# A two-stack decoder kernel in split float32r: both parts of the normed input placed at the far end of SBUF

## The chip, the cores and the metric

One core of one Trainium2 chip runs the whole program. The metric is device time in microseconds (us). A core has five engines that run their own instruction streams and meet at semaphores: TensorE (PE in the rows; its weight loads are listed apart as PEld), VectorE (DVE), ScalarE (ACT), GpSimd (POOL) and SyncE (SP), which here issues the DMAs. SBUF is the on-chip memory, 128 partitions wide; every tensor has one start address, a number of bytes inside each partition. PSUM is the small memory that TensorE writes its products to.

## The reference, cut to what matters

256 tokens of width 1024 pass through one block of a first kind (norm, input projection, a state-space mixer and banded attention side by side, output projection, then a second norm and 128 x 128 experts in the dense form below) and two blocks of a second kind (norm, projection, sparse and latent attention, output projection, then a second norm and a feed-forward part of width 4096). What is computed is set by lines such as these:

```python
def rms_norm(x, g):
    r = lax.rsqrt(jnp.mean(xf * xf, axis=-1, keepdims=True) + RMS_EPS)
    return (xf * r).astype(x.dtype) * g

proj = xn @ w_in[layer]                       # first block
h = h + (g_s5 * y_s5 + g_attn * y_attn) @ w_out[layer]
a = jnp.einsum('cd,ced->ce', xb, u_tab[eb])   # experts, up
w = gb * jax.nn.gelu(a, approximate=False)
return jnp.einsum('ce,ced->cd', w, v_tab[eb]) # experts, down
```

All inputs and outputs are float32.

## The kernel before, in words

**The split products.** A float32 product is made as three float32r products: with x = xh + xl and w = wh + wl (high part rounded, low part the rest) it adds xh·wh, xl·wh and xh·wl in one PSUM bank. A float32r matmul here takes a 128 x 128 stationary operand (loaded by an LDWEIGHTS) and streams a moving operand of 256 or 512 columns against it. In `pe.matmul(out, a, b)` the first operand, `a`, is stationary and the second, `b`, is moving. A row of a matmul names the moving operand first: `ps<-xh,wl` streams `xh` against weights from `wl`, `ps<-wh,xh` streams `wh` against a chunk of `xh` that has been loaded as the stationary operand.

**The tensors.** `xh` and `xl` hold the two parts of a normed input, 8 chunks of 256 tokens each. `wh` and `wl` hold two units each of the rounded weights and their rests. `slots` holds four units of 512 KB as they come from HBM. `early_hi` and `early_lo` (placed over the start of the arena) hold the input of the experts' query projection before its norm is applied. `mix_hi`, `mix_lo`, `hidden_hi` and `hidden_lo` are the same kind of pairs for the mixers' outputs and for the feed-forward's hidden layer. `arena` (131072 bytes per partition) holds everything else of the first block; the second kind of block lays `layer`, `mix_hi`, `mix_lo`, `hidden_hi`, `hidden_lo` and `y_out` over the same place.

**The stages, in order of the span.** 0 to 266 us: the first block's projections and mixers (`pair_product`, L537, with `xh`/`xl` moving, and with `early_hi`/`early_lo` moving from 241 us on). 266 to 653 us: 128 expert rows "up" (`up_row`, L2638, L2639 and L2643: 24 matmuls of 256 columns each, `xh`/`xl` moving). 653 to 1022 us: 128 expert rows "down" (`down_row`, L2660 and L2667: 12 matmuls of 512 columns each, `wh`/`wl` moving and a chunk of `xh`/`xl` stationary). Then twice: projections (`split_pair`, L2028, `xh`/`xl` moving), attention, `branch` (L2086, L2091), the feed-forward's up part (L2028 again) and its down part (L2329, `hidden_hi`/`hidden_lo` moving).

**The order of the work.** Every engine's stream is written out by hand, with explicit semaphores. For each unit of weights SP issues a DMA into a slot, ACT rounds it into `wh` (L184, L2376), POOL subtracts to get `wl` (L199, L2438), and PE uses the two and frees them. Nothing in this order depends on where a tensor stands.

**The placement.** Tensors are placed from the low end upwards in the order of the code, each start rounded up to a multiple of 32 bytes. The starts that matter (bytes in a partition), with the remainder by 64:

```
tensor       start    bytes    start mod 64
slots        24704    16384      0
xh           59936     8192     32
xl           68128     8192     32
wh           76320     8192     32
wl           84512     8192     32
early_hi     96832     8192      0
early_lo    105024     8192      0
mix_hi      120384     8192      0
mix_lo      128576     8192      0
hidden_hi   136768    32768      0
hidden_lo   169536    32768      0
```

A chunk of 256 tokens is 1024 bytes, so all chunks of one tensor have the remainder of its start. `xh` to `wl` stand at remainder 32 because `layer_par`, just below them, has 4056 bytes.

Of the kernel before, what the change touches and what calls it, by code (L numbers as in the profile page):

```python
# [20 lines left out]
F32R = mybir.dt.float32r  # L21
# [4 lines left out]
P = 128  # L26
T = 256
TT = T // P
D = 1024
DC = D // P  # L30
# [240 lines left out]
def build(nc, stop_after, xT, consts, par1, bias1, w1, keys, wu, wv, par2, w2, out):  # L271
    ctx = ExitStack()
    with ctx:
        def sb(name, cols, dt=F32):
            return ctx.enter_context(nc.sbuf_tensor(name, [P, cols], dt))
# [8 lines left out]
        small = sb("small", 2304)  # L284
        layer_par = sb("layer_par", LAYERS * NPAR2)

        xh, xl = sb("xh", DC * T, F32R), sb("xl", DC * T, F32R)
        wh, wl = sb("wh", 2 * SLOT, F32R), sb("wl", 2 * SLOT, F32R)
        eps, std, rst = sb("eps", 4), sb("std", T), sb("rst", T)
        row0_hi, row0_lo = (sb(n, T, F32R)[:, :] for n in ("row0_hi", "row0_lo"))  # L290
# [2608 lines left out]
```

## Time and profile before

| | |
|---|---|
| median of 3 runs | 1713.44 us (1713.36 to 1714.88) |
| profiled execution | 1710.85 us, of which span 1709.0 us |
| PE busy (matmuls) | 1638.6 us, 96% |
| PEld busy (weight loads) | 1502.8 us, 88% |
| DVE / ACT / POOL busy | 882.5 / 925.0 / 1196.7 us |
| granted TensorE clock | 0.995 of full speed |
| DMA | 280.42 MB, mean 164 GB/s |

The span runs from the first to the last instruction. Matmuls overlap each other: one lasts 280 to 400 ns by itself, while the next one starts some 120 or 227 ns after it. So the pace is read from the starts of rows in the timeline (the start of one row to the start of the next, divided by the count of the first row), or from the chain of waits, where a piece lasts until the next one begins.

### The profile page before, as it was taken

The numbers are of one execution on the slowest core, as the hardware profiler recorded it, in microseconds if no ns is written. First come the engines' busy times: TensorE is split into PE (matmuls) and PEld (weight loads), VectorE is DVE, ScalarE is ACT, GpSimd is POOL, SyncE is SP. The second block draws the span as 40 slices with busy tenths as digits, with TensorE's granted clock in tenths as the row PEclk, the third lists the DMA queues.
The fourth block names the chain that finished last, engine by engine and source line by source line (L and its number), as shares of the span: only waits on it lengthen the run. The fifth ranks groups of instructions, "written<-read, shape, count | busy, mean of one in ns | idle before, by whom it ended". The sixth has DMA issues, their size and how long they took to land.

```text
span 1709.0 us, 32062 instructions
## 1 busy us (share of the span) xinstructions
PE 1638.6 (96%) x12800; PEld 1502.8 (88%) x12800; DVE 882.5 (52%) x1817; ACT 925.0 (54%) x1553; POOL 1196.7 (70%) x500
## 2 busy tenths in 40 slices
PE   8988999999999999999999999998999998999997
PEld 7876999999999998888888888777999986789997
DVE  6988446992366667777611115876220168752101
ACT  6666655445444445555566655665553447655533
POOL 5552777888877777777888887125888762268885
PEclk9999999999999999999999999999999999999999
DMA  7431555565555555555566664513656644145663
GB/s 263 126 123 54 190 168 169 173 192 180 181 165 170 166 172 166 175 177 174 192 195 189 195 197 136 183 52 116 190 181 188 189 149 162 51 148 185 183 188 112
DMA packets 79891, 280.42 MB, mean 164 GB/s; under 512 B 8704, under 2 KB 9472, under 8 KB 79488
## 3 DMA queue, kind: packets, MB, share of 16 engines
q1 hardware_dynamic: 79744, 278.38, 52.3%
q8 instruction: 102, 1.67, 0.4%
q14 instruction: 45, 0.37, 0.1%
HBM read 277.30 MB, written 1.05 MB: 163 GB/s over the span
## 4 chain that ended last, share of the span: by engine, by line
PE 84%; DVE 6%; issue 4%; ACT 3%; POOL 2%; DMA 0%; POOLq 0%; DVEq 0%; SPq 0%; ACTq 0%
PE ps L2660 14%; PE ps L2028 13%; PE ps L2329 10%; PE ps L2638 7%; PE ps L2639 7%; PE ps L2643 7%; PE ps L2667 7%; PE ps L537 6%; POOL wl L199 2%; ACT wh L184 1%; PE ps L2624 1%; PE ps L2626 1%; PE ps L371 1%; PE ps L2152 1%; PE ps L2122 1%
## 5 line engine op out<-in xcount | busy, mean ns | idle before, releaser
L199 POOL TENSOR_TENSOR wl<-slots,wh 128x1024 fp32r<-128x1024 f32 x236 | 572.7, 2430 | 355.8 <-ACT wh L184 339.9
L2438 POOL TENSOR_TENSOR wl<-slots,wh 128x1024 fp32r<-128x1024 f32 x256 | 619.2, 2420 | 141.4 <-ACT wh L2376 139.3
L2376 ACT ACTIVATE wh<-slots 128x1024 fp32r<-128x1024 f32 x256 | 271.4, 1060 | 367.8 <-issue 237.1
L184 ACT ACTIVATE wh<-slots 128x1024 fp32r<-128x1024 f32 x236 | 249.6, 1060 | 259.7 <-PE ps L2329 105.5
L2638 PE MATMUL ps<-xh,wh 128*128 128x256 f32 x1024 | 253.7, 285 | 0.0
L2639 PE MATMUL ps<-xl,wh 128*128 128x256 f32 x1024 | 250.8, 283 | 0.0
L2639 PEld LDWEIGHTS ps<-xl,wh 128*128 128x128 f32 x1024 | 196.2, 192 | 0.0
L2638 PEld LDWEIGHTS ps<-xh,wh 128*128 128x128 f32 x1024 | 196.0, 191 | 0.1
L2660 PE MATMUL ps<-wh,xh 128*128 128x512 f32 x508 | 159.3, 395 | 0.0
L2660 PE MATMUL ps<-wh,xl 128*128 128x512 f32 x508 | 157.1, 390 | 0.0
L2537 DVE TENSOR_TENSOR small<-ps,small 128x512 f16<-128x512 f32 x128 | 87.7, 685 | 118.6 <-PE ps L2626 118.6
L2643 PE MATMUL ps<-xh,wl 128*128 128x256 f32 x1024 | 143.7, 283 | 0.6 <-POOL wl L2438 0.6
L2564 DVE TENSOR_TENSOR xl<-ps,xh 128x256 fp32r<-128x256 f32 x127 | 53.6, 422 | 167.2 <-ACT xh L2392 167.2
L2667 PE MATMUL ps<-wl,xh 128*128 128x512 f32 x508 | 136.0, 390 | 0.0
L2643 PEld LDWEIGHTS ps<-xh,wl 128*128 128x128 f32 x1024 | 132.1, 192 | 0.8 <-POOL wl L2438 0.8
L2329 PE MATMUL ps<-hidden_hi,wh 128*128 128x256 f32 x512 | 124.3, 280 | 1.9 <-POOL wl L199 1.9
L2329 PE MATMUL ps<-hidden_lo,wh 128*128 128x256 f32 x512 | 124.0, 280 | 0.0
L2667 PEld LDWEIGHTS ps<-wl,xh 128*128 128x128 f32 x508 | 95.4, 188 | 20.4
L2660 PEld LDWEIGHTS ps<-wh,xl 128*128 128x128 f32 x508 | 95.4, 188 | 20.2
L2028 PE MATMUL ps<-xh,wh 128*128 128x256 f32 x704 | 105.7, 289 | 5.5 <-ACT wh L184 3.2
L2660 PEld LDWEIGHTS ps<-wh,xh 128*128 128x128 f32 x508 | 93.2, 188 | 18.0
L2028 PEld LDWEIGHTS ps<-xh,wh 128*128 128x128 f32 x704 | 92.5, 191 | 11.7 <-issue 6.2
(386 smaller groups left out, 3067.5 us busy)
## 6 DMA issues: line engine op xcount, KB each, us to landing
slots<-w SPq DMA_DIRECT2D x260, 512.0 KB, 3.6
slots<-wu SPq DMA_DIRECT2D x128, 512.0 KB, 3.6
slots<-wv SPq DMA_DIRECT2D x128, 512.0 KB, 3.5
arena<-bias SPq DMA_DIRECT2D x1, 2048.0 KB, 8.1
h<-xT SPq DMA_DIRECT2D x4, 256.0 KB, 5.6
arena<-keys SPq DMA_DIRECT2D x1, 1024.0 KB, 8.2
yT<-y_out SPq DMA_DIRECT2D x2, 512.0 KB, 2.7
layer<-consts SPq DMA_DIRECT2D x1, 800.0 KB, 5.3
```

What stands on the lines that cost most here:

```text
L184: act.activation(self.hi[:, n % 2, :], self.slots[:, u % SLOTS, :], ACT.Copy).then_inc(self.rounded, 1)
L199: pool.tensor_tensor(self.lo[:, n % 2, :], self.slots[:, self.order[n] % SLOTS, :], self.hi[:, n % 2, :].bitcast(F32), ALU.subtract).then_ ...
L537: ins = pe.matmul(halves[j], w[:, k, :], x[:, k, :], start=(first and k == 0), stop=(last and k == DC - 1), skip_group_check=True)
L2028: ins = pe.matmul(halves[j], w[:, k, :], x[:, k, :], start=(first and k == 0), stop=(last and k == DC - 1), skip_group_check=True)
L2329: return pe.matmul(out_banks[c // 2][:, (c % 2) * T:(c % 2 + 1) * T], w[:, c * P:(c + 1) * P], x[:, u, :], start=start, stop=False, skip_g ...
L2376: act.activation(whv[:, r % 2, :], slots_v[:, r % SLOTS, :], ACT.Copy).then_inc(w_hi, 1)
L2438: pool.tensor_tensor(wlv[:, r % 2, :], slots_v[:, r % SLOTS, :], whv[:, r % 2, :].bitcast(F32), ALU.subtract).then_inc(w_lo, 1)
L2638: pe.matmul(out, hi[:, k, :], xhT[:, k, :], start=(k == 0), stop=False)
L2639: ins = pe.matmul(out, hi[:, k, :], xlT[:, k, :], start=False, stop=False)
L2643: ins = pe.matmul(out, lo[:, k, :], xhT[:, k, :], start=False, stop=(k == DC - 1))
L2660: ins = pe.matmul(psum[2 * t + half], part_a[:, tokens], hi[:, half * 512:(half + 1) * 512], start=begins, stop=False, skip_group_check=True)
L2667: ins = pe.matmul(psum[2 * t + half], a_hi[:, t * P:(t + 1) * P], lo[:, half * 512:(half + 1) * 512], start=False, stop=(row == NE2 - 1), ...
```

## The change

`xh` and `xl` are allocated from the other end of SBUF. Nothing else in the code changes.

```diff
-        xh, xl = sb("xh", DC * T, F32R), sb("xl", DC * T, F32R)
+        xh, xl = (ctx.enter_context(nc.sbuf_tensor(n, [P, DC * T], F32R, side="right")) for n in ("xh", "xl"))
         wh, wl = sb("wh", 2 * SLOT, F32R), sb("wl", 2 * SLOT, F32R)
```

What stood above `xl` moves down by 16384 bytes, and the two tensors fill the last 16384 bytes:

```
tensor       start before   start now   mod 64 before, now   mod 128 before, now
xh              59936        221152          32, 32               32, 96
xl              68128        212960          32, 32               32, 96
wh              76320         59936          32, 32               32, 32
wl              84512         68128          32, 32               32, 32
std             92736         76352           0, 0                64, 64
row0_hi         94784         78400           0, 0                64, 64
early_hi        96832         80448           0, 0                64, 64
arena           96832         80448           0, 0                64, 64
mix_hi         120384        104000           0, 0                64, 64
hidden_hi      136768        120384           0, 0                64, 64
```

`h`, `slots`, `cst`, `p1`, `small` and `layer_par`, below `xh`, stay where they were. The instructions of each engine and their order are the same as before, so no piece of the order is shown.

## Rows read from the trace of the kernel before

**Rows 1.** The page: time and busy shares, then the clock of 40 slices.
```profile
span 1709.0 us, 32062 instructions
PE 1638.6 (96%) x12800; PEld 1502.8 (88%) x12800; DVE 882.5 (52%) x1817; ACT 925.0 (54%) x1553; POOL 1196.7 (70%) x500
...
PEclk9999999999999999999999999999999999999999
```

**Rows 2.** The page, chain that ended last: shares by engine and by line.
```profile
PE 84%; DVE 6%; issue 4%; ACT 3%; POOL 2%; DMA 0%; POOLq 0%; DVEq 0%; SPq 0%; ACTq 0%
PE ps L2660 14%; PE ps L2028 13%; PE ps L2329 10%; PE ps L2638 7%; PE ps L2639 7%; PE ps L2643 7%; PE ps L2667 7%; PE ps L537 6%; POOL wl L199 2%; ACT wh L184 1%; PE ps L2624 1%; PE ps L2626 1%; PE ps L371 1%; PE ps L2152 1%; PE ps L2122 1%
```

**Rows 3.** Waits of PE, 262 to 1025 us: line, releaser, total us, times, longest.
```profile
PE ps L2609 <- ACT arena L2406: 1.2, 1, 1.2
PE ps L2643 <- POOL wl L2438: 0.6, 1, 0.6
```

**Rows 4.** Lines of PE by form: count, then busy us, mean ns, idle before.
```profile
L2638 PE MATMUL ps<-xh,wh 128*128 128x256 f32 x1024 | 253.7, 285 | 0.0
...
L2028 PE MATMUL ps<-xh,wh 128*128 128x256 f32 x704 | 105.7, 289 | 5.5 <-ACT wh L184 3.2 <-ACT xh L1551 2.1
...
L537 PE MATMUL ps<-xh,wh 128*128 128x256 f32 x368 | 57.5, 300 | 13.8 <-ACT xh L651 7.5 <-DVE arena L958 2.6 <-ACT wh L184 1.6
```

**Rows 5.** Chain in order of time, its long pieces: start us, us, what.
```profile
200.07 1.87 PE ps L1189 x16
...
870.08 1.81 PE ps L2660 x8
...
872.80 1.81 PE ps L2660 x8
...
1194.25 78.98 PE ps L2028 x656
...
1606.01 81.99 PE ps L2329 x696
```

**Rows 6.** Timeline of PE, 1250 to 1276 us: start us, us, line, operands, count.
```profile
1250.03 1.12 PE L2028 MATMUL ps<-xh,wh 128*128 128x256 f32 x8
...
1272.11 1.12 PE L2028 MATMUL ps<-xh,wl 128*128 128x256 f32 x8
1273.07 0.28 PE L2329 MATMUL ps<-hidden_hi,wh 128*128 128x256 f32 x1
...
1274.96 1.10 PE L2329 MATMUL ps<-hidden_hi,wl 128*128 128x256 f32 x8
1275.90 0.28 PE L2329 MATMUL ps<-hidden_hi,wh 128*128 128x256 f32 x1
```

**Rows 7.** Timeline of PE, 218 to 262 us.
```profile
231.38 1.12 PE L537 MATMUL ps<-xh,wl 128*128 128x256 f32 x8
...
240.02 1.12 PE L537 MATMUL ps<-xh,wl 128*128 128x256 f32 x8
...
250.75 1.10 PE L537 MATMUL ps<-early_hi,wl 128*128 128x256 f32 x8
...
253.55 1.09 PE L537 MATMUL ps<-early_hi,wl 128*128 128x256 f32 x8
```

**Rows 8.** Chain, 300 to 340 us: first and last of 12 like pieces.
```profile
306.47 0.96 PE ps L2643 x8
...
338.15 0.96 PE ps L2643 x8
```

**Rows 9.** Lines of DVE and of ACT by form that write the split pairs.
```profile
L1759 DVE SCALAR_TENSOR_TENSOR xl<-ps,layer_par,xh 128x256 fp32r<-128x256 f32 x32 | 12.9, 473 | 0.0
L1870 DVE SCALAR_TENSOR_TENSOR mix_lo<-ps,layer_par,mix_hi 128x256 fp32r<-128x256 f32 x16 | 7.7, 482 | 13.1 <-ACT mix_hi L1637 13.0
...
L1551 ACT ACTIVATE xh<-ps,layer_par 128x256 fp32r<-128x256 f32 x32 | 12.3, 483 | 4.6 <-DVE ps L1973 1.9 <-DVE ps L1751 1.5 <-DVE ps L1772 1.2
L1637 ACT ACTIVATE mix_hi<-ps,layer_par 128x256 fp32r<-128x256 f32 x16 | 7.5, 469 | 0.0
```

## The prediction

> **What bounds the kernel now.** The page comes first: PE is busy 96% of the 1709.0 us span, and its clock stays in the top tenth in all 40 slices [rows 1]. The chain that ended last agrees: 84% of it is PE, and the lines that stream `xh` or `xl` (L2028, L2638, L2639, L2643, L537) hold 13 + 7 + 7 + 7 + 6 = 40% of the span [rows 2]. In the expert stages, 763 us long, PE's waits for POOL's rest and ACT's copies come to under 2 us [rows 3]. So a matmul that is made shorter or longer by a few ns moves the end, and nothing else about the placement does, since no instruction and no wait is moved.
>
> **The pace of the matmuls.** The next view is the one that the change is about: how long after one matmul the next one starts. The timeline between 1250.03 and 1272.11 us shows 23 groups of 8 matmuls with `xh` or `xl` moving; 22.08 / 184 is 120.0 ns each [rows 6]. The same at another time: 8.64 us for 72 matmuls between 231.38 and 240.02, again 120.0 ns [rows 7]. The expert rows come 31.68 / 11 = 2.88 us apart, 24 matmuls each, 120.0 ns [rows 8]. The 656 of the long piece take 78.98 us, 120.4 ns with a few small ones among them [rows 5].
>
> Then the same engine, with the same weights in `wh` and `wl`, streams something else, and it gets quicker. With `early_hi` and `early_lo` moving, 24 matmuls take 253.55 - 250.75 = 2.80 us, 116.7 ns [rows 7]. With `mix_hi`/`mix_lo` (L1189) 16 take 1.87 us, 116.9 ns. With `hidden_hi`/`hidden_lo` 696 take 81.99 us, 117.8 ns [rows 5]; right at the seam, where `xh` gives way to `hidden` at 1273.07, the last group of 8 takes 0.96 us, the next 16 matmuls take 1.89 us, 118.1 ns, and the 8 behind them 0.94 us, 117.5 ns [rows 6]. The difference is 2.2 ns (120.0 - 117.8) to 3.3 ns (120.0 - 116.7). It comes with the moving tensor, not with the time, the weights or the line of code: L537 shows both paces within 20 us.
>
> What do the tensors at 120.0 ns have in common? Two things, by the table of starts. They stand low (`xh`, `xl` below 76320; the quick ones from 96832 up). And their starts leave 32 by 64, while every quick one leaves 0. The change alters the first and keeps the second: 221152 and 212960 both leave 32. That is the whole question of this prediction.
>
> **The change part by part.**
>
> 1. *`xh` and `xl` as moving operand.* Counts: 3 x 1024 up the experts, 3 x 704 at L2028, 3 x 368 at L537 (of each three only the first form is shown, the other two have its count), 6288 in all [rows 4]. On the chain they hold 40% of 1709, some 684 us; less the 192 with `early` moving (22 us at 116.7 ns), that is 662 / 0.120 = about 5,500. If the pace goes with the remainder by 64, the term is 0. If it goes with height, it is 5,500 x 2.2 to 3.3 ns = 12 to 18 us less. I take 0, for this reason: a boundary by height would have to lie between `wl`'s last chunk (84512 + 8192 = 92704) and the start of `early_hi` at 96832, whose groups are quick; that leaves out 98304 (96 KiB), the only round address nearby, since `early_hi`'s first chunk lies wholly below it. A boundary by banks shared with the weights doesn't fit either: `xh`'s first five chunks end below 65536 and its last two lie above it, together with `xl` and `wh`, and a group of 8, which runs through all these chunks, takes 8 x 120.0 ns, with no room for a quick chunk in it. The remainder by 64 separates the two kinds with nothing left over. This I read as a cause that is likely, not shown: both marks are confounded in this trace.
>
> 2. *`xh` and `xl` as stationary operand*, in the 1524 "down" matmuls of 512 columns. 12 of them take 872.80 - 870.08 = 2.72 us, 226.7 ns each [rows 5]. Streaming is `wh`/`wl`, remainder 32 before and after. Taken: 0. If moving and stationary operand must only lie far apart to be quick, 1524 x 2.2 to 3.3 = 3 to 5 us less.
>
> 3. *`wh`, `wl` 16384 lower.* 16384 is a multiple of 64, so remainders stay; and `hidden` (136768 to 202304) keeps one pace over 65536 bytes against the same weights, so distance as such does nothing. Taken: 0.
>
> 4. *`early`, `mix`, `hidden`, `arena` 16384 lower.* `mix` and `hidden` go to 104000 and up, addresses at which quick tensors stand now. `early` goes to 80448, among the addresses of the 120.0 ns kind: by height its 192 matmuls would lose 3.3 ns each, 0.6 us. By remainder nothing. Taken: 0.
>
> 5. *The writers.* ACT and DVE write `xh` and `xl` at the far end now. The nearest rows: the DVE form takes 473 ns into `xl` and 482 into `mix_lo`, ACT 483 into `xh` and 469 into `mix_hi` [rows 9]: within 3% of each other, of opposite sign, low against high. Even 10 ns more in 32 of each would be 0.3 us on either engine, and both wait for PE in most of the span. Taken: 0, bounds -0.3 and +0.6 us.
>
> 6. *POOL, DMA.* `slots` stays; POOL reads `slots` and `wh` and writes `wl` as before, and PE waits for it 0.6 us in the expert stages [rows 3]. Taken: 0.
>
> The sum is 0: the profiled execution of 1710.85 us (span 1709.0 and 1.85 around it) would be 1710.85 again, and the median of the three runs, 2.59 us above it, stays 1713.4 us. The forecast's own range is 1711.0 to 1716.5, from the bounds of steps 4 and 5 and the spread of the runs shown.
>
> A page of the Trainium skill bears on this in two ways. SBUF — State Buffer, section "Who interferes with whom", says that PE never waits for another engine's access; by that rule moving `xh` out of the neighbourhood of `wh` gives nothing, which is the forecast. The same page, section "Door 1: The DMA port swizzle", gives SBUF lines of 16 bytes; every start here is a multiple of 32, so by that rule no moving tensor should differ from another, and the sum would be 0 as well. But the rows do show a difference of 2.2 to 3.3 ns between tensors, so the rule is at least too coarse here, and the measurement decides.
>
> **The rivals.**
>
> *A. Height or distance decides: faster.* `xh`/`xl` at 212960 and up would run like `early` or `hidden`. For it: all quick tensors stand above 96832, all at 120.0 ns below 92704, without exception. Against it: no round boundary fits between, and `hidden`'s even pace over 64 KiB shows no dependence on height. Price: 12 to 18 us less, and 3 to 5 more if the down rows join: 1690 to 1701.5, in the middle of the first part 1698 us. PE could use it all: per expert row it would want 24 x 117 = 2.81 us, and POOL's wait of 0.6 us in all shows that it is not close behind.
>
> *B. A finer remainder decides, and the new one is worse: slower.* `xh` and `xl` now leave 96 by 128 and start 32 bytes before a multiple of 1024 (221152 + 32 = 216 x 1024), so each 1024-byte chunk begins with a sliver of 32 bytes and then crosses that boundary, in each of the 6288 moving reads. If the start of a stream pays one step for the sliver, the nearest size for a step is the difference between the kinds, 2.2 to 3.3 ns: 5,500 x that is 12 to 18 us more, 1725.5 to 1731.6, in the middle 1728 us. It shows beyond no change from 0.6 ns a matmul (3.4 us / 5,500). For it: some fine remainder evidently matters, and the remainder by 128 changes here. Against it: at remainder 32 the sliver by 64 is just as short already, and it is by 64 that the kinds separate cleanly.
>
> **How the numbers follow.** Forecast 0.69, A 0.21, B 0.10. What a measurement of this kernel can tell from no change is about 0.2%, 3.4 us. The forecast's 0.69 gives 0.66 within, 0.02 faster and 0.01 slower; A is wholly faster, B wholly slower: 0.23, 0.66, 0.11. The predicted time is the forecast's, 1713.4. The range has to leave out no more than 0.2: with B outside (0.10), it takes in the forecast's own and A down to 1696, which leaves the end with the down rows outside.
>
> **What would show it right or wrong.** In the profile after, the groups of 8 with `xh` or `xl` moving are to be 0.96 us apart, the up rows 2.88 us, the down rows 2.72 us, and `early` and `hidden` as before (0.93 to 0.94 us for 8). If the groups with `xh` come at 0.93 or 0.94 us and `early`'s at 0.96, height decides and A holds; if they come above 0.97 us, B. If the groups keep 0.96 us and the time still moves by more than 3.4 us, the reason is outside of everything weighed here: then ACT's or DVE's means for writing `xh` and `xl`, or the waits of PE, must have moved.

## The result: 1682.2 us, 1.9% faster, and the profile after

The changed kernel takes 1682.16 us (median of 5 runs, 1680.56 to 1684.81) against 1714.06 us of before in the same comparison: ratio 0.9815, 95% interval 0.9803 to 0.9827. The forecast was no change, 1713.4 us, with a range down to 1696; the time fell 14 us below that range. The sign is that of rival A, the reason is nearer to rival B's, and the size is neither's.

The page of the profile after, against [rows 1]: the clock and the counts are the same, the span is 30.2 us shorter and PE's busy time 33.2 us.

```profile
span 1678.8 us, 32062 instructions
PE 1605.4 (96%) x12800; PEld 1466.3 (87%) x12800; DVE 884.0 (53%) x1817; ACT 925.6 (55%) x1553; POOL 1195.5 (71%) x500
...
PEclk9999999999999999999999999999999999999999
```

PE's waits in the expert stages (262 to 1008 us), against [rows 3]: nothing was waited away.

```profile
PE ps L2609 <- ACT arena L2406: 1.2, 1, 1.2
PE ps L2643 <- POOL wl L2438: 0.7, 1, 0.7
```

The timeline of PE in the first block, against [rows 7] (start us, us, line, operands, count):

```profile
225.78 1.07 PE L537 MATMUL ps<-xh,wh 128*128 128x256 f32 x8
...
238.47 1.07 PE L537 MATMUL ps<-xh,wl 128*128 128x256 f32 x8
...
249.10 1.10 PE L537 MATMUL ps<-early_hi,wl 128*128 128x256 f32 x8
...
251.90 1.09 PE L537 MATMUL ps<-early_hi,wl 128*128 128x256 f32 x8
```

From 225.78 to 238.47 us there are 14 groups of 8 with `xh` or `xl` moving: 12.69 / 112 = 113.3 ns each, where it was 120.0. That is quicker than any such stretch in the trace before. With `early` moving, now at 80448 among the low addresses, 24 matmuls take 2.80 us, 116.7 ns, exactly as before. Rival A asked for 0.93 or 0.94 us for 8 with `xh` and for 0.96 us with `early`; they take 0.91 and 0.93. So a low address does not slow `early`. Whether a large distance from the weights speeds up `xh` is left for the experiments.

The chain of waits, against [rows 5] and [rows 8]: one piece of 8 in each up row (first and last of nine), two down rows, then the long pieces of the layers.

```profile
314.37 0.91 PE ps L2643 x8
...
336.13 0.91 PE ps L2643 x8
...
870.05 1.83 PE ps L2660 x8
...
872.79 1.83 PE ps L2660 x8
...
1175.45 74.63 PE ps L2028 x656
...
1576.52 81.22 PE ps L2329 x696
```

An up row takes 21.76 / 8 = 2.72 us, not 2.88; a down row 2.74 to 2.75, not 2.72; the 656 matmuls of L2028 take 74.63 us instead of 78.98; the 696 of `hidden` 81.22 instead of 81.99. The starts of the up stage and of the down stage behind it come from the view of single lines (min/median/max duration in ns, then first and last start in us). Before:

```profile
L2638 PE MATMUL ps<-xh,wh x1024: 278/283/385, 266.3 to 658.8; 128*128 128x256 f32 x171
L2660 PE MATMUL ps<-wh,row_hi x4: 395/396/500, 660.9 to 662.2; 128*128 128x512 f32 x4
```

After:

```profile
L2638 PE MATMUL ps<-xh,wh x1024: 276/276/384, 264.8 to 638.7; 128*128 128x256 f32 x171
L2660 PE MATMUL ps<-wh,row_hi x4: 392/396/498, 640.7 to 642.0; 128*128 128x512 f32 x4
```

The up stage shrank from 394.6 (660.9 - 266.3) to 375.9 us: 18.7 of the 30.2. (It ends at 660.9 us before the change, and the down stage at 1028, some 6 to 8 us later than the rough stage limits given with the kernel.) The two pieces of 656 (one in each layer, both as long as the one shown) gave 2 x 4.35 = 8.7, the stage ahead of the experts 1.5, the two feed-forward down parts 0.8 each. The down stage gave back 2.5 (from the starts of its first and last matmul). What is left, about 2 us, lies in the rest of the two layers and is not broken down.

### The profile page after: what moved, and what is told of

The parts are those of the page before. It is cut to its first block, busy times and chain, and to the rows that moved or that the text cites. A ratio compares the mean times of both kernels' runs of the same rounds, so it can differ in the third digit from the quotient of the medians.

```text
span 1678.8 us, 32062 instructions
## 1 busy us (share of the span) xinstructions
PE 1605.4 (96%) x12800; PEld 1466.3 (87%) x12800; DVE 884.0 (53%) x1817; ACT 925.6 (55%) x1553; POOL 1195.5 (71%) x500
## 4 chain that ended last, share of the span: by engine, by line
PE 83%; DVE 6%; issue 4%; ACT 3%; POOL 3%; DMA 0%; POOLq 0%; DVEq 0%; SPq 0%; ACTq 0%
PE ps L2660 14%; PE ps L2028 13%; PE ps L2329 10%; PE ps L2638 7%; PE ps L2667 7%; PE ps L2639 7%; PE ps L2643 7%; PE ps L537 6%; POOL wl L199 2%; ACT wh L184 1%; PE ps L2624 1%; PE ps L2626 1%; PE ps L371 1%; PE ps L2152 1%; PE ps L2122 1%
## 5 line engine op out<-in xcount | busy, mean ns | idle before, releaser
L2638 PE MATMUL ps<-xh,wh 128*128 128x256 f32 x1024 | 242.0, 279 | 0.0
L2639 PE MATMUL ps<-xl,wh 128*128 128x256 f32 x1024 | 238.8, 276 | 0.0
L2638 PEld LDWEIGHTS ps<-xh,wh 128*128 128x128 f32 x1024 | 192.3, 188 | 0.1
L2639 PEld LDWEIGHTS ps<-xl,wh 128*128 128x128 f32 x1024 | 192.3, 188 | 0.0
L2643 PE MATMUL ps<-xh,wl 128*128 128x256 f32 x1024 | 137.2, 276 | 0.7 <-POOL wl L2438 0.7
L2643 PEld LDWEIGHTS ps<-xh,wl 128*128 128x128 f32 x1024 | 125.6, 188 | 1.2 <-POOL wl L2438 0.9
L2660 PEld LDWEIGHTS ps<-wh,xh 128*128 128x128 f32 x508 | 93.2, 188 | 18.7
L2028 PE MATMUL ps<-xh,wh 128*128 128x256 f32 x704 | 101.6, 283 | 5.5 <-ACT wh L184 3.2
L2028 PEld LDWEIGHTS ps<-xh,wh 128*128 128x128 f32 x704 | 88.7, 188 | 11.7 <-issue 6.2
```

What stands on the lines that cost most here:

```text
L2028: ins = pe.matmul(halves[j], w[:, k, :], x[:, k, :], start=(first and k == 0), stop=(last and k == DC - 1), skip_group_check=True)
L2638: pe.matmul(out, hi[:, k, :], xhT[:, k, :], start=(k == 0), stop=False)
L2639: ins = pe.matmul(out, hi[:, k, :], xlT[:, k, :], start=False, stop=False)
L2643: ins = pe.matmul(out, lo[:, k, :], xhT[:, k, :], start=False, stop=(k == DC - 1))
L2660: ins = pe.matmul(psum[2 * t + half], part_a[:, tokens], hi[:, half * 512:(half + 1) * 512], start=begins, stop=False, skip_group_check=True)
```

## The experiments

The theory after the result: the pace goes with the low bits of the starts. Differences are those of `xh`'s start less `wh`'s, by 256; `xl` and `wl` stand 8192 bytes beside them and give the same. `early`, `mix` and `hidden` less `wh` leave 32 by 256, before and after the change; in e3_w96 and e4_both96 they leave 224, in b1 to b3 192.

### e1_low96: low end, 64 bytes up

```diff
+        sb("pad_x", 16)
         xh, xl = sb("xh", DC * T, F32R), sb("xl", DC * T, F32R)
+        sb("pad_w", 240)
         wh, wl = sb("wh", 2 * SLOT, F32R), sb("wl", 2 * SLOT, F32R)
```

> xh and xl stay at the low end, right below the weights, but start at 60000 and 68192: remainder 96 by 128 instead of 32. Everything above moves up by 1024 bytes and keeps its remainders. Theory R (the low bits of the starts set the pace, height nothing): the groups of 8 with xh or xl moving come 0.91 us apart (113.3 ns, as in the changed kernel), hidden stays near 117, the time is the changed kernel's, 1680 to 1685 us. Theory H (height, or distance from the weights): 0.96 us (120.0 ns) as before, 1713 us. If low bits above 128 count (the changed kernel has 992 by 1024, this one 608), the pace is something else again, 113 to 120 ns.

Measured: 1708.65 us, ratio 0.9968 (0.9955 to 0.9980). Neither theory's number came, but the third case named did, another pace. The chain, one piece in each up row, then one in each down row:

```profile
344.99 0.94 PE ps L2645 x8
347.81 0.94 PE ps L2645 x8
...
850.85 1.87 PE ps L2662 x8
853.65 1.87 PE ps L2662 x8
```

Up rows 2.82 us apart (117.8 ns a matmul), down rows 2.80 us (233 ns). So 64 bytes at the low end do change the pace of both kinds, which height can't explain, but the remainder by 128 is not the whole rule. The slower down rows take most of the gain back: that stage lasts 375.3 us from first to last start, against 366.5. And `hidden`, whose difference to `wh` is 32 as before, runs at 120.0 ns here, where it ran at 117.8:

```profile
1608.18 83.53 PE ps L2331 x696
```

### e2_top32: far end, the old low bits

```diff
+        ctx.enter_context(nc.sbuf_tensor("pad_top", [P, 112], F32, side="right"))
         xh, xl = (ctx.enter_context(nc.sbuf_tensor(n, [P, DC * T], F32R, side="right")) for n in ("xh", "xl"))
```

> xh and xl at the far end of SBUF as in the changed kernel, but 448 bytes lower, at 220704 and 212512: remainder 32 by 128 and 544 by 1024, the same low bits as before the change; weights and arena as in the changed kernel. Theory R: the groups of 8 come 0.96 us apart again, 120.0 ns, and the time is that of before, 1712 to 1716 us. Theory H: 0.91 us and 1680 to 1685 us.

Measured: 1713.47 us against 1713.45, ratio 1.0000 (0.9991 to 1.0009). The chain shows the old pace to the last digit:

```profile
343.54 0.96 PE ps L2644 x8
346.42 0.96 PE ps L2644 x8
```

This kernel does everything that the change says: both parts at the far end, weights and arena 16384 bytes lower. It differs from the changed kernel in 448 bytes, and it gains nothing. The place is not the cause.

### e3_w96 and e4_both96: which operand's low bits

```diff
         xh, xl = sb("xh", DC * T, F32R), sb("xl", DC * T, F32R)
+        sb("pad_w", 16)
         wh, wl = sb("wh", 2 * SLOT, F32R), sb("wl", 2 * SLOT, F32R)
+        sb("pad_a", 240)
```

> xh and xl exactly where they stood before the change (remainder 32 by 128); wh and wl 64 bytes higher, at 76384 and 84576, remainder 96. It asks whether the moving operand's low bits count alone or the two operands' together. Theory R1 (the moving one alone): xh groups stay at 0.96 us; the down rows, where wh and wl stream, gain what xh gained, 6.7 ns a matmul: 12 of them 2.64 us instead of 2.72, some 10 us less, 1703 us. Theory R2 (the difference of the two starts by 128, 0 before and 64 in the changed kernel): xh groups 0.91 us, down rows 2.75 us as in the changed kernel, 1682 us. Theory H: no change, 1713 us.

```diff
+        sb("pad_x", 16)
         xh, xl = sb("xh", DC * T, F32R), sb("xl", DC * T, F32R)
         wh, wl = sb("wh", 2 * SLOT, F32R), sb("wl", 2 * SLOT, F32R)
+        sb("pad_a", 240)
```

> xh, xl, wh and wl all 64 bytes higher at the low end, all with remainder 96 by 128. Theory R1 (the moving operand alone): xh groups 0.91 us and down rows 2.64 us, 1713 - 31 - 12 = 1670 us. Theory R2 (the difference of the two starts, which is 0 again): xh groups 0.96 us, 1713 us. Theory H: 1713 us.

e3_w96: 1698.97 us, 0.9914 (0.9901 to 0.9928). `xh` and `xl` did not move by a byte, and their matmuls became quicker. e4_both96: 1716.12 us, 1.0013 (1.0005 to 1.0022): with all four moved by the same 64 bytes the pace is 120 ns again (up rows 2.88 us). So it is the difference of the two starts that counts, and R1 and H are out. That e4_both96 is some 2.7 us slower than before, and not equal to it, fits the other tensors: at the difference 224 its 696 matmuls of `hidden` take 82.38 us instead of 81.99, and those of `mix` and `early` 118.3 ns instead of 116.7 to 117.8. e3_w96 missed R2's 1682 us by 17 us, and shows why in its chain, the same 656 matmuls in its first and in its second layer:

```profile
1187.81 77.53 PE ps L2030 x656
...
1519.11 74.63 PE ps L2030 x656
```

77.53 us is a pace of 117.8 ns with a few small ones among them, 74.63 us is 113.3. Same code, same addresses, one execution: at this difference the pace can settle at either value. In the trace some 60% of its matmuls with `xh` or `xl` moving in uninterrupted stretches run at 117.8 ns.

### m1_grid: matmuls alone

```python
for i in range(count):                       # 40 of 256 columns or 24 of 512
    k = i % 8 if cols == 256 else i // 2 % 8
    m = i % 8 * 256 if cols == 256 else i % 2 * 512
    ins = pe.matmul(ps[:, 512 * (i % 2):512 * (i % 2) + cols], made[still][:, k * P:(k + 1) * P],
                    made[moving][:, m:m + cols], start=True, stop=True, skip_group_check=True)
```

> A kernel of matmuls alone (it leaves the whole computation out and copies its input to its output). 40 float32r matmuls of 256 columns with tensor x moving and tensor w stationary, for each of 8 starts of x (remainders 0, 32, 64, 96, 128, 192, 256, 512 by 1024: xa to xh) and 4 starts of w (0, 32, 64, 96: wa to wd), each of the 32 twice in another order, an idle pause between; then 24 matmuls of 512 columns for the first 4 x 4. Theory R2 (the difference of the two starts by 128 decides): 120.0 ns where it is 0, 113.3 ns where it is 64, 117 to 118 where it is 32 or 96, the same in each row of equal difference, and 128, 256 and 512 do as 0. Theory of 64 (the moving start's remainder by 64, from the prediction): xb and xd 120 ns, the rest 117. Theory of traffic (the pace comes from the other engines' and the DMAs' accesses beside it): all 32 alike here, since nothing else runs. If the pace can settle in more than one value at one placement, the two times of a pair differ.

The timeline of PE; 40 matmuls of 256 columns (moving, stationary), then 24 of 512:

```profile
35.90 5.05 PE L2949 MATMUL ps<-xa,wa 128*128 128x256 f32 x40 [0.34 <-ACT scratch L2939]
...
46.68 4.82 PE L2949 MATMUL ps<-xa,wc 128*128 128x256 f32 x40 [0.37 <-ACT scratch L2939]
...
105.74 4.98 PE L2949 MATMUL ps<-xd,wb 128*128 128x256 f32 x40 [0.42 <-ACT scratch L2939]
...
175.53 4.99 PE L2949 MATMUL ps<-xg,wc 128*128 128x256 f32 x40 [0.41 <-ACT scratch L2939]
...
256.18 4.82 PE L2949 MATMUL ps<-xg,wc 128*128 128x256 f32 x40 [0.43 <-ACT scratch L2939]
...
379.27 5.74 PE L2949 MATMUL ps<-xa,wa 128*128 128x512 f32 x24 [0.36 <-ACT scratch L2939]
391.63 5.86 PE L2949 MATMUL ps<-xa,wc 128*128 128x512 f32 x24 [0.39 <-ACT scratch L2939]
...
460.12 5.78 PE L2949 MATMUL ps<-xd,wb 128*128 128x512 f32 x24 [0.34 <-ACT scratch L2939]
```

The first matmuls of a group start further apart (the first two some 222 ns), and the last one's own 0.28 us is in the row, so a row divided by 40 gives too much. Behind the first eight, from start to start in the trace, the row of 5.05 us has 120.0 ns, 4.82 has 113.3, 4.98 and 4.99 have 117.8. All 64 groups of 256 columns, by the moving start less the stationary one:

```
difference by 256     0       32      64      96      128     160      192              224
ns                  120.0   116.7   117.8   120.1   118.7   117.4*   113.3 or 117.8   118.4
(* 118.6 in two groups of eight)
```

With nothing else at work the values are those of the whole kernel (116.7 ns at 32 is the pace of `early`), so the theory of traffic is out, and so is my remainder by 64 of the moving start (xa at 0 gives 120.0 with wa, 113.3 with wc). The pair xg and wc, difference 192, shows 117.8 ns at 175.53 and 113.3 at 256.18 us. R2 fails in its detail: 96 gives 120 ns and not 117 to 118, and xe (128) with wa gives 118.7, not 120.0, while xg (256) and xh (512) with wa give 120.0. The period is 256, not 128.

### e5_low992: the changed kernel's low bits, at the low end

```diff
+        sb("pad_x", 112)
         xh, xl = sb("xh", DC * T, F32R), sb("xl", DC * T, F32R)
+        sb("pad_w", 144)
         wh, wl = sb("wh", 2 * SLOT, F32R), sb("wl", 2 * SLOT, F32R)
```

> xh and xl at the low end, at 60384 and 68576, weights at 77344 and 85536: all low ten bits as in the changed kernel (992 and 544 by 1024), only the height is that of before. Theory R (low bits alone, up to 1024): the changed kernel's pace, 113.3 ns up the experts, and its time, 1680 to 1685 us. Theory H joined to R (the far end is needed too): 117 ns or more, as in the run with remainder 96 at the low end, 1705 to 1715 us. Theory M (with a difference of 64 the pace can settle at 113.3 or at 117.8 ns, and small things choose): anything from 1682 to 1712 us, and runs of one kernel that differ by several us.

Measured: 1691.26 us (1686.17 to 1698.12), ratio 0.9871 (0.9848 to 0.9894): theory M's spread. The chain, one piece in each up row, shows a row in which the pace changes:

```profile
298.75 0.91 PE ps L2645 x8
301.47 0.91 PE ps L2645 x8
304.19 1.16 PE ps L2645 x8
307.24 0.94 PE ps L2645 x8
```

Rows 2.72 us apart up to 304.19; in that row PE held for a moment just ahead of the products with `wl` (1.16 us instead of 0.91; the view of waits names no releaser for it), and behind it the rows are 2.82 us apart. Then the transposes of the chosen keys ahead of row 50 interrupt PE, and it settles at 113.3 ns again:

```profile
414.99 0.95 PE ps L2645 x8
415.94 0.66 PE ps L2691 x6
418.43 0.91 PE ps L2645 x8
421.15 0.91 PE ps L2645 x8
```

In the traces of the twelve whole kernels no uninterrupted stretch with one moving tensor changes its pace on the way.

### m2_odd64: seven tries of each odd multiple of 64

The grid kernel with other starts, 24 matmuls a group and pauses of different length.

> Matmuls alone again (the computation is left out, the input copied out). All placements but the last group have a difference of 64 by 128 between the moving and the stationary start: x at 64, 192, 320, ... 960 by 1024 (xa to xh), w at 0, 128, 256 (wa, wb, wc); 24 matmuls of 256 columns for each of the 24 pairs, seven times in different orders, with pauses of different length between. Then wd (64 by 1024, difference 0 by 128) with each x, twice. Theory M256 (the difference by 256 sorts them: 64 always settles at 117.8 ns, 192 can settle at 113.3): of the seven groups of a pair with difference 64 by 256 all show 117.8, of those with 192 most show 113.3 and a few 117.8. Theory M (any difference of 64 by 128 can settle at either, by the moment of the start): both values in each pair, whatever the difference by 256. Theory P (placement alone): each pair has one value, seven times. With wd 120.0 ns always, in all three.

The timeline of PE, pair xa (64) and wb (128), difference 192 by 256, four of its seven groups; then two of xc (320) and wc (256), difference 64:

```profile
39.86 3.02 PE L2950 MATMUL ps<-xa,wb 128*128 128x256 f32 x24 [0.35 <-ACT scratch L2940]
...
63.85 3.09 PE L2950 MATMUL ps<-xc,wc 128*128 128x256 f32 x24 [0.37 <-ACT scratch L2940]
...
122.64 3.10 PE L2950 MATMUL ps<-xc,wc 128*128 128x256 f32 x24 [0.43 <-ACT scratch L2940]
...
168.13 3.01 PE L2950 MATMUL ps<-xa,wb 128*128 128x256 f32 x24 [0.35 <-ACT scratch L2940]
...
247.50 3.00 PE L2950 MATMUL ps<-xa,wb 128*128 128x256 f32 x24 [0.43 <-ACT scratch L2940]
...
313.17 3.10 PE L2950 MATMUL ps<-xa,wb 128*128 128x256 f32 x24 [0.36 <-ACT scratch L2940]
```

A row of 3.00 to 3.02 us has 113.3 ns from start to start behind its first eight, one of 3.09 to 3.10 has 117.8. Counted over all groups:

```
difference by 256    113.3 ns    117.8 ns    118.7 ns    120.0 ns
192                     67          17
 64                      4          80
  0                                                          8
128                                              8
```

M256 is right in the main, and M has its share: the other value turns up at either difference, rarely at 64, one time in five at 192. That wd gives 120.0 ns always was a miss: with half of the x its difference is 128 by 256, and there it is 118.7.

### e6_top128 and e7_top256: the period in the whole kernel

e6_top128 has a pad of 32 float32 columns at the far end, e7_top256 one of 64, in e2's way.

> The changed kernel with xh and xl another 128 bytes lower, at 221024 and 212832: remainder 96 by 128 as before, so the difference to wh by 128 stays 64, by 256 it is 64 and no longer 192. Theory M256: the groups of 8 with xh or xl moving come 0.94 us apart (117.8 ns) throughout, and the time is 1713.5 less 5,500 x 2.2 ns, some 1700 to 1708 us. Theory R2 (by 128 alone): 0.91 us and 1680 to 1685 us. Theory M: between the two, and different from run to run.

> The changed kernel with xh and xl 256 bytes lower, at 220896 and 212704: the difference to wh is 192 by 256 as in the changed kernel, by 512 it is 192 and no longer 448. Theory 256: the changed kernel's pace, 113.3 ns with some stretches at 117.8, 1680 to 1692 us. Theory 512 or more (a larger period sorts the pace): 117.8 ns or more throughout and 1700 us or more.

e6_top128 (difference 64): 1707.90 us, 0.9970 (0.9958 to 0.9982). e7_top256 (difference 192): 1684.18 us, 0.9831 (0.9818 to 0.9845). The chain of e6, two up and two down rows:

```profile
342.58 0.94 PE ps L2644 x8
345.41 0.94 PE ps L2644 x8
...
851.02 1.87 PE ps L2661 x8
853.82 1.87 PE ps L2661 x8
```

These are e1's values, and e1 has the same difference, 64, at the other end of SBUF. e7 has the changed kernel's: 2.72 us up, 2.75 us down. 128 bytes take most of the gain away, 256 bytes leave it, at a time 2 us above the changed kernel's. e6 also shows that the value at one difference isn't settled by the pace at which a stage is entered: like e1_low96 it comes into its last feed-forward down part at 117.8 ns, with `hidden` at the difference 32 in both, and takes 116.7 ns where e1 takes 120.0:

```profile
1603.12 81.22 PE ps L2330 x696
```

### b1_all192, b2_down0, b3_down0: what follows from it

b1 brings `early`, `mix` and `hidden` to the difference 192 too; b2 and b3 move the down rows' activations inside `xh` and `xl`, in three places of the code:

```diff
         row0_hi, row0_lo = (sb(n, T, F32R)[:, :] for n in ("row0_hi", "row0_lo"))
+        sb("pad_a", 40)                                    # b1, b2, b3
...
-    ... xhT[:, 4 + row % 4, :], xlT[:, 4 + row % 4, :]
+    ... xh[:, (4 + row % 4) * T - 16:(5 + row % 4) * T - 16], xl[...]   # b2: 64 bytes lower
+    ... xh[:, (4 + row % 4) * T - 48:(5 + row % 4) * T - 48], xl[...]   # b3: 192 bytes lower
```

> The changed kernel with the arena, and so early, mix and hidden, 160 bytes higher: their difference to wh and wl becomes 192 by 256 as that of xh and xl, instead of 32. 2368 more matmuls of 256 columns could go from some 117 to 113.3 ns. Theory M256: hidden, mix and early groups of 8 at 0.91 us wherever they settle low, 1682 less 2368 x 3.5 ns = 8 us, 1674 us; if the feed-forward part enters at 117.8 and stays there, no gain. Theory that the differing pace of hidden comes from something else than the placement: hidden stays at 116 to 118 ns, 1682 us.

> As the run before, and in the down stage the activations stand 64 bytes lower inside xh and xl, so that the stationary operand has the difference 0 by 128 to the weights that stream past it. By the grid of matmuls alone 512 columns take 226.7 ns at difference 0 and 228.9 at 64: the down rows come 2.72 us apart instead of 2.75, 1524 x 2.2 ns = 3.4 us less than the run before, some 1671 us. If the 226.7 against 228.9 ns is no matter of placement but of what else runs, both runs have the same down stage.

> As b1_all192 (arena 160 bytes higher than in the changed kernel), with the down stage's activations 192 bytes lower inside xh and xl instead of 64: their start less that of wh is 0 by 256, where b2_down0 had 128 and 233 ns a matmul. Theory 256 (the difference by 256 sorts the pace of both kinds of matmul): 512 columns at 226.7 ns, down rows 2.72 us apart, the down stage 366.5 us as before the change and 2.5 us shorter than b1_all192's: some 1674.5 us. Theory that moving the activations out of the chunks' grid costs in itself (the reads or the writes at shifted places): 233 ns and 1687 us again.

b1: 1677.42 us, 0.9784 (0.9770 to 0.9799). `hidden` gained as forecast, in its chain:

```profile
1577.57 78.89 PE ps L2330 x696
```

78.89 / 696 = 113.3 ns. Part of it was lost in the profiled execution by 20 up rows at 117.8.

b2: 1686.96 us, 0.9840 (0.9826 to 0.9854), slower than b1: a miss. I had reckoned by 128; by 256 the down rows now had the difference 128. The down stage lasts 374.9 us against b1's 369.0; another 3 us are up rows that settled at 117.8 ns in its profiled execution. Its chain, two down rows 2.80 us apart:

```profile
850.90 1.87 PE ps L2661 x8
853.70 1.87 PE ps L2661 x8
```

b3, with the difference 0 by 256: 1676.52 us, 0.9777 (0.9764 to 0.9791), down rows 2.72 us apart as before the change:

```profile
852.17 1.81 PE ps L2661 x8
854.89 1.81 PE ps L2661 x8
```

So moving them costs nothing in itself; the difference does. b3 has the lowest median of all, but its interval overlaps b1's; that it gains is read from the down stage, 366.5 us instead of 369.0.

The whole in one table (difference of the activations' start less the weights', by 256; activations move in the up rows and stand still in the down rows):

```
difference    up row us    down row us    seen in
0                2.88          2.72       before, e2, e4 (b3 in the down rows)
64               2.82          2.80       e1, e6
128               -            2.80       b2 in the down rows
192           2.72 or 2.82     2.75       after, e3, e5, e7, b1 (b2, b3 in the up rows)
```

## Why the prediction was wrong, point by point

- **What bounds the kernel: right.** PE alone; a few ns in the distance of two matmuls moved the end, no wait changed, and no other engine followed.
- **The pace of the matmuls: read rightly, and the useful part.** That two identical matmuls with the same weights run at 120.0 and at 116.7 ns by the tensor that moves was the trace's whole hint.
- **The step that failed: "The remainder by 64 separates the two kinds with nothing left over. This I read as a cause that is likely, not shown", in step 1, and with it "If the pace goes with the remainder by 64, the term is 0".** The term was 0 in the sum; what was measured is some 30 us less. I looked for a property of the moving tensor alone, since the weights were the same in both kinds. But the same weights make the difference of the starts vary with the moving tensor just as well. Before, `xh` - `wh` is -16384, 0 by 256, and `early`, `mix` and `hidden` less `wh` are 32 by 256; the change makes the first 192 (221152 - 59936 = 161216) and leaves the second. Both starts stood in the table. e4_both96 against e3_w96 shows the difference to be the quantity, m1_grid that nothing else has to run for it.
- **The size.** I priced the other cases by the nearest rows, 2.2 to 3.3 ns a matmul. The change brought 6.7 in steady stretches (120.0 to 113.3), a pace that no row of before had. Over the up stage it is 18.7 us / 3072 = 6.1 ns, since the first matmuls behind an interruption gain less. The range's low end hung on these 3.3 ns.
- **Steps 2 and 3, taken as 0.** The down rows lost: 226.7 to 228.9 ns, 2.5 us over the stage, and the grid alone gives the same two values at the differences 0 and 192 (stationary start less moving). Step 3 took `hidden`'s even pace over 65536 bytes as proof that distance does nothing. But its chunks stand 1024 bytes apart and all have the same difference to the weights by 256, so that row could not speak about the low bits of a distance.
- **Steps 4 to 6: right but for `hidden`.** `early` keeps 116.7 ns at 80448. `hidden`, taken as 0, gained 0.8 us in each layer with its difference unchanged (117.8 to 116.7 ns); the prediction had put 116.7 and 117.8 ns down as one kind, and they were a second hint, of a pace that can settle at more than one value. The sums of busy time of ACT, DVE and POOL moved by 0.6, 1.5 and 1.2 us.
- **Rival A** had the sign and not the cause: e2_top32 does all it asks for and gains nothing, e5_low992 and e3_w96 gain without it. Its sign came true by luck. **Rival B** had the right kind of cause, a finer remainder than 64 that the change alters, but of the moving start alone, which e3_w96 and e4_both96 exclude, and took it for a loss. A forecast that says "some fine remainder matters, and this change alters one" owed that case more than 0.10, with both signs.
- **The two reads of PE.** In m1_grid, where ACT, DVE, POOL and the kernel's DMAs stand still while the matmuls run, the pace goes from 113.3 to 120.0 ns with nothing but the difference of the two starts. The Trainium skill, SBUF — State Buffer, section "Who interferes with whom", gives PE two read ports, one for the moving operand and one for the weight load, independent of each other, and says that PE waits for no one. By that rule the difference should do nothing; it does, and the measurement decides.

What stays open: what inside the memory or the engine has the period of 256 bytes, and what chooses between 113.3 and 117.8 ns at the difference 192, and between 116.7, 117.8 and 120.0 ns at 32. That the two reads hinder each other is a reading that fits; the runs show the dependence, not the circuit.

## What to carry to other kernels

When float32r matmuls run back to back, each with its own weight load, look at the time from one start to the next. Where the same shape runs at two paces, as here, the thing to compute is the moving operand's start less the stationary one's, by 256. A small pad can then do what moving a tensor across SBUF seems to do: 64 bytes between `xl` and `wh` (e3_w96) took 14.5 us off, and the far end with the old difference (e2_top32) nothing. Before crediting a move with a gain, repeat it with the old low bits kept: e2_top32 is that control, and one such run rules the place out. Try the pad on every pair of operands that a tensor is part of, since what speeds up the up rows can slow the down rows (e1_low96). Only float32r matmuls of 256 and 512 columns with 128 x 128 weights were measured.

## What the runs showed of the hardware that was not expected

- The distance between matmuls of 256 columns depends on the moving start less the stationary one by 256: in m1_grid and m2_odd64, 120 ns at 0 and 96, 118.7 at 128, 117.8 at 64 (80 of 84), 113.3 (67 of 84) or 117.8 ns at 192. For 512 columns, by the stationary start less the moving one: 226.7 ns at 0, 228.9 at 192, 233 at 64 (all in m1_grid), and 233 at 128 (b2_down0).
- At one placement the pace can settle at two values, keeps its value through hundreds of matmuls (656 in e3_w96), and changes it at an interruption or where the moving tensor changes. The kernels differ in their spread from run to run: e5_low992 by 12 us over 5 runs and e1_low96 by 10 over 6, against 3 us of e2_top32 over 11. That this comes from the settling is likely, not shown: each kernel has one trace.
- The feed-forward down parts of the changed kernel and of e2_top32 have all operands at the same addresses, and take 81.22 and 81.99 us for the same 696 matmuls. They are entered from 113.3 and from 120.0 ns. The pace of entry is not the whole rule: e1_low96 and e6_top128 both enter from 117.8 ns, at the same difference 32, and take 83.53 and 81.22 us.
